# Who multiplies the modulation tiles by the condition: eight VectorE steps, or ScalarE in place with one VectorE sum

## The reference, cut to what matters

```python
c_act = jax.nn.silu(c)
mod = (jnp.einsum('bd,dn->bn', c_act, w_ada[l]) + b_ada[l]).reshape(b, N_SUB, 3, D_MODEL)
h = modulate(x, norm_w[l, 0], mod[:, 0, 0], mod[:, 0, 1])
x = x + 0.5 * mod[:, 0, 2][:, None, :] * swiglu(h, ffn_w13[l, 0], ffn_w2[l, 0])
h = modulate(x, norm_w[l, 1], mod[:, 1, 0], mod[:, 1, 1])
y = hybrid_mixer(h, ...)
x = x + mod[:, 1, 2][:, None, :] * y
h = modulate(x, norm_w[l, 2], mod[:, 2, 0], mod[:, 2, 1])
x = x + 0.5 * mod[:, 2, 2][:, None, :] * swiglu(h, ffn_w13[l, 1], ffn_w2[l, 1])
# second block, its own condition and its own weight of 6144 columns
mod = (jax.nn.silu(c) @ ada_w[i] + ada_b[i])[:, None, :]
mod_c = (jax.nn.silu(c_ctx) @ ada_w[i][:, :n_ctx_mod] + ada_b[i][:n_ctx_mod])[None, None, :]
```

## Time and profile before

| | |
|---|---|
| median of three executions | 1704.6 us |
| the profiled execution | 1707.38 us |
| its span, first to last instruction | 1705.6 us |
| mean granted TensorE clock | 0.997 |
| TensorE matmuls busy | 1681.9 us (99%) |
| VectorE busy | 1145.5 us (67%) |
| ScalarE busy | 690.2 us (40%) |
| the six steps on line 1984 | 147.5 us (x360) |

### The profile page before, as it was taken

The page is one execution under the profiler, slowest core; times in us unless marked ns, Lnnn a source line. Parts: engine busy times, 40 slices in busy tenths (PEclk is TensorE's granted clock), DMA queues, the critical chain, the costliest instruction groups (busy, mean ns, idle before and its releaser), DMA issues.

```text
span 1705.6 us, 24579 instructions
## 1 busy us (share of the span) xinstructions
PE 1681.9 (99%) x8956; PEld 1408.0 (83%) x8956; DVE 1145.5 (67%) x2122; ACT 690.2 (40%) x1048; POOL 67.4 (4%) x56
## 2 busy tenths in 40 slices
PE   7999999999999999999999999999999999999998
PEld 5788888888878868897888888888868988989897
DVE  3778578655655686469969973469675558656563
ACT  4421222234236573354222334342466443626262
POOL 0000000011000000200000000200000200000002
PEclk9999999999999999999999999999999999999999
DMA  9866567332523302537666642354200232434231
GB/s 330 259 203 197 178 201 212 108 103 54 145 74 98 99 1 75 171 106 219 188 205 188 175 116 80 112 169 113 87 1 15 86 112 74 119 85 124 85 108 50
DMA packets 355674, 218.59 MB, mean 128 GB/s; under 512 B 8544, under 2 KB 353668, under 8 KB 355588
## 3 DMA queue, kind: packets, MB, share of 16 engines
q1 hardware_dynamic: 355356, 217.37, 43.8%
q10 hardware_dynamic: 232, 0.09, 0.0%
HBM read 215.34 MB, written 2.11 MB: 127 GB/s over the span
## 4 chain that ended last, share of the span: by engine, by line
PE 95%; DVE 2%; DMA 1%; issue 1%; ACT 0%; SPq 0%; POOL 0%; DVEq 0%; ACTq 0%; POOLq 0%
PE bank L777 24%; PE bank L779 24%; PE bank L778 24%; PE bank L1314 2%; PE bank L1315 2%; PE bank L1313 2%; PE bank L1039 2%; PE bank L1023 1%; PE bank L955 1%; PE bank L959 1%; PE bank L956 1%; PE bank L1101 1%; PE bank L1273 1%; PE bank L1075 1%; DMA GBUF<-in_w_ada 1%
## 5 line engine op out<-in xcount | busy, mean ns | idle before, releaser
L1471 ACT ACTIVATE W_HI<-RAW 128x1024 fp32r<-128x1024 f32 x278 | 292.3, 1056 | 463.2 <-PE bank L779 401.5
L777 PE MATMUL bank<-H_HI,W_HI 128*128 128x512 f32 x1090 | 426.1, 391 | 3.9 <-DVE W_LO L1955 3.8
L778 PE MATMUL bank<-H_LO,W_HI 128*128 128x512 f32 x1090 | 424.7, 390 | 0.0
L779 PE MATMUL bank<-H_HI,W_LO 128*128 128x512 f32 x1090 | 424.7, 390 | 0.0
L1955 DVE TENSOR_TENSOR W_LO<-RAW,W_HI 128x1024 fp32r<-128x1024 f32 x254 | 311.3, 1226 | 95.3 <-ACT W_HI L1471 92.1
L777 PE MATMUL bank<-A_HI,W_HI 128*128 128x512 f32 x714 | 279.7, 392 | 0.0
L778 PE MATMUL bank<-A_LO,W_HI 128*128 128x512 f32 x714 | 278.2, 390 | 0.0
L779 PE MATMUL bank<-A_HI,W_LO 128*128 128x512 f32 x714 | 278.2, 390 | 0.0
L777 PEld LDWEIGHTS bank<-H_HI,W_HI 128*128 128x128 f32 x1090 | 204.7, 188 | 49.3 <-issue 5.1
L779 PEld LDWEIGHTS bank<-H_HI,W_LO 128*128 128x128 f32 x1090 | 204.7, 188 | 42.4
L778 PEld LDWEIGHTS bank<-H_LO,W_HI 128*128 128x128 f32 x1090 | 204.8, 188 | 42.2 <-issue 0.2
(11 more groups left out here) (435 smaller groups left out, 2313.5 us busy)
## 6 DMA issues: line engine op xcount, KB each, us to landing
RAW<-in_ffn_w SPq DMA_DIRECT2D x116, 512.0 KB, 4.8
GBUF<-in_w_ada SPq DMA_DIRECT2D x32, 1024.0 KB, 7.4
RAW<-in_mlp_w SPq DMA_DIRECT2D x64, 512.0 KB, 4.1
RAW<-in_w_in SPq DMA_DIRECT2D x57, 512.0 KB, 3.9
GBUF<-in_ada_w SPq DMA_DIRECT2D x24, 1024.0 KB, 7.2
RAW<-in_w_out SPq DMA_DIRECT2D x16, 512.0 KB, 4.0
RAW<-in_ffn_w SPq DMA_DIRECT2D x16, 384.0 KB, 3.4
PBUF<-in_w_ada SPq DMA_DIRECT2D x4, 1024.0 KB, 10.9
```

Of the source, the lines that this page charges most:

```text
L777: pe.matmul(dst, w_hi, x_hi, start=first and i == 0, stop=False)
L778: pe.matmul(dst, w_hi, x_lo, start=False, stop=False)
L779: mm = pe.matmul(dst, w_lo, x_hi, start=False, stop=last and i == len(blocks) - 1)
L1471: act.activation(strip_of(W_HI, slot), strip_of(RAW, slot), ACT.Copy).then_inc(hi_ready, 1)
```

## The change

It adds `scale_gem` to ScalarE: it waits for a tile to land and multiplies each of its eight chunks by the condition's column in place, eight activations of 128x256, and counts `gem_scaled`. On VectorE `scaled_tile` waits for that and sums the eight chunks in one tensor_reduce over a view of the tile in which the chunk index is innermost (neighbours 256 elements apart) into GACC; transpose and reduce follow as before. 44 of the 52 tiles go this way. The 8 odd tiles of the second FFN's up parts, which two conditions need, stay as they were. On ScalarE an up turn now has as many chunks as on VectorE (four, or six in the third part of the first FFN), the first FFN's turns and the down parts with tiles are written out, and lines shift by a few numbers.

```diff
+        def scaled_by_act(f, up, g):
+
+            return not (f and up and g % 2)
...
 # @block.scalar
+            def scale_gem(slot, vec):
+
+                g = GBUF[:, slot * KC * GEM:(slot + 1) * KC * GEM]
+                act.wait_ge(gem_in[slot], gem_of[slot].add(16))
+                for k in range(KC):
+                    at = slice(k * GEM, (k + 1) * GEM)
+                    ins = act.activation(g[:, at], g[:, at], ACT.Copy, scale=CSIL[:, vec + k:vec + k + 1])
+                ins.then_inc(gem_scaled, 1)
...
-            def ffn_up(u0, chunks):
-
-                def turn(it, u0, c0, split=0):
-                    for p in range(2):
-                        first = split and p == 0
-                        for j in (2 * p, 2 * p + 1):
+            def ffn_up(u0, f, chunks, ups):
+
+                per = up_turn(ups, chunks)
+                vec = C_2 if f else C_1
+
+                def turn(it, split=0):
+                    for c in range(per):
+                        p, g = c % 2, u0 + 2 * c
+                        first = split and c == 0
+                        for j in (2 * c, 2 * c + 1):
                             if not first:
-                                split_next(u0, it, j)
...
                         if first:
                             split_next(u0, it, split)
-                        act.wait_ge(bank_free, it * RING + (g + 2 + RING))
...
+                        if ups and c < GEM_RING:
+                            if scaled_by_act(f, True, c):
+                                scale_gem(c, vec)
+                            else:
+                                gem_of[c].add(16)
+                        act.wait_ge(bank_free, it * 2 * per + (g + 2 + RING))
+                        act.activation(chunk(A_HI, it * per + c), HF[:, p * S:(p + 1) * S], ACT.Copy).then_inc(ahi_ready, 1)
...
-            def down(u0, squares=None, halves=False):
-
+            def down(u0, squares=None, halves=False, gem_vec=None):
+
+                if gem_vec is not None:
+                    for j in range(KC):
+                        split_next(u0, 0, j)
+                        if j in GEM_AFTER:
+                            scale_gem(GEM_AFTER.index(j), gem_vec)
+                    return
...
 # @block.vector
+                return folded(at)
+
+            def folded(at):
+
+                after(dve.transpose(GTURN[:, :], GACC[:, 0:GEM]))
...
+            def scaled_tile(slot, at):
+
+                g = GBUF[:, slot * KC * GEM:(slot + 1) * KC * GEM]
+                dve.wait_ge(gem_scaled, scaled.add())
+                after(dve.tensor_reduce(GACC[:, 0:GEM], g.rearrange("p (k n) -> p n k", k=KC), AX.X, ALU.add))
+                return folded(at)
+
+            def gem_step(slot, seq_no, vec, at, also, by_act):
...
+                if by_act:
+                    scaled_tile(slot, at).then_inc(gem_done, 1)
+                    return
+                dve.wait_ge(gem_in[slot], landed)
...
-                            gem_step(g, seq_no + g, vec, tile(0, g))
+                            gem_step(g, seq_no + g, vec, tile(0, g), None, True)
```

More of the change, by code:

```diff
@@ L275, in block_pair_kernel @@
         gem_done = sem("gem_done")
+        gem_scaled = sem("gem_scaled")
         pe_gem_in = [sem(f"pe_gem_in{i}") for i in range(4)]
@@ L1471, in split_hi, with split_next @@
                 act.activation(strip_of(W_HI, slot), strip_of(RAW, slot), ACT.Copy).then_inc(hi_ready, 1)
-            def split_next(u0, it, j):
+            def split_next(u0, it, j, per=RING):
                 u = u0 + j + LEAD
-                if not isinstance(it, int) or it * RING + u < STRIPS:
-                    split_hi(it * RING + u, u % RING, it + u // RING)
+                if not isinstance(it, int) or it * per + u < STRIPS:
+                    split_hi(it * per + u, u % RING, it * (per // RING) + u // RING)
+            gem_of = [Tally(gem_in[i]) for i in range(GEM_RING)]
+            for t in gem_of:
+                t.add(16)
+            def scale_gem(slot, vec):
[5 more added lines that the diff above has]
+                ins.then_inc(gem_scaled, 1)
             silu, ahi, un = Tally(silu_ready), Tally(ahi_ready), Tally(un_ready)
@@ L1536, in turn @@
                             split_next(u0, it, split)
-                        act.wait_ge(bank_free, it * RING + (g + 2 + RING))
-                        act.activation(chunk(A_HI, it * 2 + (c0 + p)), HF[:, p * S:(p + 1) * S], ACT.Copy).then_inc(ahi_ready, 1)
+                        if ups and c < GEM_RING:
[5 more added lines that the diff above has]
+                        act.activation(chunk(A_HI, it * per + c), HF[:, p * S:(p + 1) * S], ACT.Copy).then_inc(ahi_ready, 1)
                 if u0 == U_FFN0:
-                    turn(0, u0, 0, split=1)
-                    with loop(act, chunks // 2 - 1) as it:
-                        turn(it, u0 + RING, 2)
-                else:
-                    with loop(act, chunks // 2) as it:
-                        turn(it, u0, 0)
-            def down(u0, squares=None, halves=False):
+                    turn(0, split=1)
+                    for it in range(1, chunks // per):
+                        turn(it)
+                else:
+                    with loop(act, chunks // per, *([(t, 16) for t in gem_of] if ups else [])) as it:
+                        turn(it)
+            def down(u0, squares=None, halves=False, gem_vec=None):
[5 more added lines that the diff above has]
+                    return
                 if squares is not None:
@@ L1892, in _ @@
             for i, (_, chunks) in enumerate(FFN_PARTS):
-                ffn_up(u, chunks)
+                ffn_up(u, 0, chunks, GEM_PLAN[0][i][0])
                 u += 2 * chunks
-                down(u, 0 if i == 2 else None, True)
+                down(u, 0 if i == 2 else None, True, C_1 if GEM_PLAN[0][i][2] else None)
                 u += KC
@@ L1900, in _ @@
             for i, (_, chunks) in enumerate(FFN_PARTS):
-                ffn_up(u, chunks)
+                ffn_up(u, 1, chunks, GEM_PLAN[1][i][0])
                 u += 2 * chunks
@@ L1910, in _ @@
                                    scale=1.0 / D).then_inc(ctx_std, 1)
-                down(u, 2 * (KC - 1) if i == 2 else None)
+                down(u, 2 * (KC - 1) if i == 2 else None, gem_vec=C_2 if GEM_PLAN[1][i][2] else None)
                 u += KC
@@ L1964, in _ @@
             hsq, hstd, rinv, half = Tally(head_sq), Tally(head_std), Tally(rinv_ready), Tally(half_done)
-            gem_seq = KC + 2
+            scaled = Tally(gem_scaled)
+            gem_seq, scaled_seq = KC + 2, 2
             h_own, alo_own = Tally(h_ready), Tally(alo_ready)
@@ L2095, in ffn_up @@
                 gem, per = [], up_turn(ups, chunks)
+                by_act = [scaled_by_act(also is not None, True, g) for g in range(GEM_RING)]
                 if ups:
-                    gem = [(t, 16) for t in gem_of] + [(seq, 4 * gem_seq + (2 * (gem_seq + 1) if also is not None else 0))]
+                    gem = [(t, 16) for t in gem_of] + [(scaled, by_act.count(True)),
+                                                       (seq, by_act.count(True) * scaled_seq + by_act.count(False) * (2 * gem_seq + 1))]
                 def turn(it, skip=False):
@@ L2113, in turn @@
                         if ups and c < GEM_RING:
-                            gem_step(c, it * GEM_RING + (seq_no + c), vec, tile(it, c), also if c % 2 else None)
+                            gem_step(c, it * GEM_RING + (seq_no + c), vec, tile(it, c), also, by_act[c])
                 if u0 == U_FFN0:
```

8 lines of the change are left out of this document (3 added, 5 removed).

## The result

The changed kernel takes 1713.1 us (median of six executions, 1711.16 to 1715.52) against 1704.6 us; the ratio is 1.0046, with an interval of 1.0036 to 1.0056. The profiled execution took 1712.65 us for a span of 1710.8 us. So it is slower by 8.5 us, where 6.3 were forecast; the time lies inside the range on record (1706 to 1716) and 0.1 us above the range of the case called likeliest (1708.5 to 1713).

What follows compares the result with a forecast made beforehand. TensorE was taken as the bound, busy for 99% of the span. Delays of 3.6 us in the first FFN and 2.7 us in the second sum to 6.3 us: 1704.6 + 6.3 = 1710.9 us, range 1706 to 1716.

Steps and rivals of the forecast that it cites:

- the case called likeliest: Whole kernel: a wide step costs and the clock holds; 1710.9 us, own range 1708.5 to 1713, chance 0.48.
- the two places: Chunk 0 of the first and second FFN, where TensorE waits for strip 5's split; 3.6 and 2.7 us later.
- the delay of A_LO: Chunk 0 of each FFN: ScalarE's pass ahead of A_HI makes A_LO 2.8 us later (first), 1.9 us (second).
- First FFN, +3.6: Chunk 0, first FFN: A_LO 2.8 us later plus a tile 0.8 us longer delay strip 5 by 3.6 us.
- Second FFN, +2.7: Chunk 0, second FFN: A_LO 1.9 us later plus a tile 0.8 us longer delay strip 5 by 2.7 us.
- The reduce, T: VectorE's sum of a tile over the wide view: 4.2 us taken, bounds 2.3 and 4.8 us.
- No new wait elsewhere: Outside the waits ahead of strip 5 in both FFNs, TensorE was to get no new wait, so nothing was added.
- VectorE's two-chunk stretch: Second FFN's up parts: split to split two chunks later grows from 20.3 to 21.1 us, within TensorE's 21.8.
- The clock: Rival: the stall ahead of strip 5 lowers TensorE's clock for some 7 us, costing 3.7 us: 1714.6 us, chance 0.19.
- The kept pace: Rival: VectorE's reduce keeps its pace on the wide view, taking 2.3 us: 1707.1 us, chance 0.22.
- VectorE as the bound: Rival: a reduce above 4.9 us makes VectorE too slow in the second FFN's up parts; 1722 us at 6, chance 0.07.
- the relief: Rival: VectorE's lighter work reaches TensorE and its 1.8 us of waits in the FFNs go: 1702.8 us, chance 0.04.

Runs made afterwards that it cites:

- the eight steps: The changed kernel with ScalarE's pass kept, but VectorE doing its old eight multiply steps and the add on the tile: 1710.6 us, ratio 1.0030.
- the three additions: The changed kernel with VectorE's sum made of three contiguous additions in place of the reduce over the wide view: 1708.0 us, ratio 1.0016.
- The best version: The changed kernel with three contiguous additions for the sum and VectorE's split of the next strip ahead of the tile: 1702.8 us, ratio 0.9989.
- the price run: The changed kernel with 24 extra VectorE reduces and copies at various steps behind the first FFN's last tile, to measure their prices; its run time means nothing.

## Why the prediction was right, and where it was off

**Where.** Right: the two places, the wait for the split of strip 5 behind a later A_LO and a longer tile, and the sign. The kernel with chunk 0 by VectorE shows that nothing else in the FFNs lost time but the fold. Too narrow: the delay of A_LO as the cause. With the pass behind A_HI, A_LO was early again and the waits were as long (2.84 and 3.13 us).

**First FFN, +3.6.** Measured +2.95. The pass took 3.29 us for 3.4, and A_LO came 2.6 us later for 2.8. The tile grew by 3.84 + 0.04 - 3.48 = 0.4 for 0.8.

**Second FFN, +2.7.** Measured +2.09: 1.8 for 1.9 from A_LO, 0.4 for 0.8 from the tile. The wait at strip 7 stayed, as said.

**The reduce, T.** The largest mis-sized term of the sum: 4.2 us for 3.85, which makes 2 x 0.35 = 0.7 of the 1.2 us too much. I had carried ScalarE's 0.94 ns per element over to VectorE; it is 0.64. The choice between the rows (a copy that kept its pace out of PSUM, a copy that did not in SBUF) was right: in SBUF the price is paid from 16 bytes on from one operand to the next.

**ScalarE.** A row with a pointer for a bias gave the price of one with a pointer for the scale: 497 ns and a pitch of 0.40, for 508 and 0.42.

**"No new wait elsewhere": wrong.** I tested the cover of ScalarE's passes and of VectorE's two-chunk stretch, which measured 822.03 - 801.29 = 20.7 us for 21.1, and not the end of a down part, where the last tile's count is waited for by the fold. VectorE works down a backlog there; each tile is 0.4 us longer, and the last one begins 3.9 us before TensorE's last strip ends, where it had been 4.7. The last tile's first step, before and now:

```profile
996.69 0.61 DVE L1981 TENSOR_SCALAR GACC<-GBUF,CSIL 128x256 f32<-128x256 f32 x2
```

```profile
1001.53 3.83 DVE L2036 TENSOR_REDUCE GACC<-GBUF 128x256 f32<-128x2048 f32 x1
```

TensorE's last strip ended at 1001.4 and 1005.4 us. The price of that step, which I had at nothing, is 1.1 us; with the eight steps or the three additions the wait is gone.

**The clock.** I gave it 0.19 and 3.7 us as a rival. It is part of what happened, at half that size: 1.7 us, behind one of the two stalls. The prediction also said that no stall of this length stands in the trace of before; one does, 6.54 us ahead of TensorE's first matmul for the load of CROW, but no work of TensorE comes before it. Forecast and rival were not alternatives; a forecast of a stall of nearly 4 us should have carried the fall in its likeliest case.

**The other rivals.** The kept pace, VectorE as the bound and the relief fell: T is 3.85 us. The best version reached the relief's bound of 1702.8 us, but not by the sum behind it: the 1.8 us of waits went, 0.81 came at strip 11, and most of the rest is the 0.5 us that the vanished waits give back beyond their brackets.

In sum: 6.3 - 1.2 (sizes) + 1.1 (fold) + 1.7 (clock) = 7.9 us. That the forecast came within 2.2 us of the median owes something to luck: the sizes were too large, and two terms, 2.8 us, were left at nothing.

## What to carry to other kernels

Work that is moved to an idle engine still stands in somebody's order: look at what is queued behind it and who waits for that, first at the places where a stage begins and the bound engine is already waiting. Here a sum over an outer axis in one instruction, with operands 1 KB apart, took 3.85 us, and three contiguous additions 2.4, even though these read and write more; both ways are worth a try. And a short wait ahead of a busy stretch may only show that the helping engine is behind over the whole stretch: taking that wait away alone moved it some strips on, and less work for the helper shortened it there.

## What was not expected of the hardware

- The reduce in the kernel takes 3.85 us, the same one in the price run, where TensorE and ScalarE mostly stood, 3.59 us. What makes the 0.25 us was not tried.
- The price of a wide step differed by engine and operation: 0.64 ns per element for VectorE's reduce, 0.37 for its copy, where ScalarE's copy gave 0.94.
- A stall of 1.81 us was followed by 2 x (0.40 + 0.45) = 1.7 us of lost clock, nearly as much as the stall itself, while one of 2.84 us was followed by none.
